# Five weight slots whose low part replaces the loaded block, unrolled stage loops, and other first transfers

## What is computed

```python
def swiglu(x, w_in, w_out):
    gate, up = jnp.split(x @ w_in, 2, axis=-1)
    return (jax.nn.silu(gate) * up) @ w_out
...
    x = x + 0.5 * swiglu(rmsnorm(x, ffn1_norm_g[l]), ffn1_w_in[l], ffn1_w_out[l])
```

## Time and profile before

| | |
|---|---|
| median of 3 runs | 1616.91 us (1616.56 to 1619.34) |
| the profiled execution's own time | 1615.48 us |
| its span, first to last instruction | 1613.8 us |
| TensorE busy | 1598.9 us, 99% |
| VectorE busy | 1220.4 us, 76% |
| ScalarE busy | 806.4 us, 50% |
| weight loads, 1 MB each | 269 on SyncE's queue, median 4.9 us from issue to landing |
| modulation loads, 1 MB each | 72 on GpSimd's queue, median 7.5 us |
| params, consts | 1474 KB, 280.5 KB |

### The profile page before, as it was taken

The page is one execution under the profiler, slowest core; times in us unless marked ns, Lnnn a source line. Parts: engine busy times, 40 slices in busy tenths (PEclk is TensorE's granted clock), DMA queues, the critical chain, the costliest instruction groups (busy, mean ns, idle before and its releaser), DMA issues.

```text
span 1613.8 us, 33803 instructions
## 1 busy us (share of the span) xinstructions
PE 1598.9 (99%) x14163; PEld 1577.0 (98%) x14163; DVE 1220.4 (76%) x1382; ACT 806.4 (50%) x892; POOL 48.2 (3%) x81
## 2 busy tenths in 40 slices
PE   9999999999999999999999999999999999999998
PEld 9999999999999999999998999999999998899998
DVE  7788786676778878887768788867889578774544
ACT  5434567654644354444567554345443456654343
POOL 0000000000000000000000000000000010000000
PEclk9999999999999999999999999999999999999999
DMA  8788644444568865888343369874898545345551
GB/s 334 282 305 306 225 178 170 150 157 160 182 258 291 314 229 206 334 320 310 140 176 131 131 238 343 309 284 157 297 339 322 187 144 196 132 157 209 182 199 61
DMA packets 51067, 365.04 MB, mean 226 GB/s; under 512 B 5793, under 2 KB 5921, under 8 KB 7073
## 3 DMA queue, kind: packets, MB, share of 16 engines
q1 hardware_dynamic: 40176, 287.03, 48.9%
q0 software_dynamic: 10368, 75.50, 12.9%
q10 hardware_dynamic: 432, 1.20, 0.2%
HBM read 362.65 MB, written 1.05 MB: 225 GB/s over the span
## 4 chain that ended last, share of the span: by engine, by line
PE 95%; DVE 2%; ACT 1%; DMA 1%; issue 1%; DVEq 0%; SPq 0%; ACTq 0%
PE bank L261 53%; PE bank L319 27%; PE bank L283 3%; PE bank L302 2%; PE bank L253 1%; PE bank L2172 1%; PE bank L406 1%; DVE wlo L192 1%; PE bank L417 1%; DMA raw<-stream_in 0%; PE bank L1675 0%; PE bank L2218 0%; PE bank L2124 0%; PE bank L2142 0%; PE bank L451 0%
## 5 line engine op out<-in xcount | busy, mean ns | idle before, releaser
L192 DVE TENSOR_TENSOR wlo<-raw,whi 128x2048 fp32r<-128x2048 f32 x254 | 581.0, 2289 | 187.0 <-ACT whi L184 186.3
L261 PE MATMUL bank<-xh,whi 128*128 128x256 f32 x2544 | 707.6, 278 | 1.6 <-DVE wlo L192 1.6
L261 PE MATMUL bank<-xh,wlo 128*128 128x256 f32 x2544 | 704.1, 277 | 0.0
L261 PE MATMUL bank<-xl,whi 128*128 128x256 f32 x2544 | 704.0, 277 | 0.0
L184 ACT ACTIVATE whi<-raw 128x2048 fp32r<-128x2048 f32 x253 | 482.5, 1913 | 260.4 <-PE bank L261 147.7
L261 PEld LDWEIGHTS bank<-xh,whi 128*128 128x128 f32 x2544 | 478.2, 188 | 3.1 <-DVE wlo L192 2.0
L261 PEld LDWEIGHTS bank<-xl,whi 128*128 128x128 f32 x2544 | 478.0, 188 | 0.1
L261 PEld LDWEIGHTS bank<-xh,wlo 128*128 128x128 f32 x2544 | 477.9, 188 | 0.0
L319 PE MATMUL bank<-hid_hi,whi 128*128 128x256 f32 x1056 | 293.3, 278 | 0.0
L319 PE MATMUL bank<-hid_hi,wlo 128*128 128x256 f32 x1056 | 292.2, 277 | 0.0
L319 PE MATMUL bank<-hid_lo,whi 128*128 128x256 f32 x1056 | 292.2, 277 | 0.0
(11 more groups left out here) (398 smaller groups left out, 1904.7 us busy)
## 6 DMA issues: line engine op xcount, KB each, us to landing
raw<-stream_in SPq DMA_DIRECT2D x269, 1024.0 KB, 4.9
mod_raw<-mod_in POOLq DMA_DIRECT2D x72, 1024.0 KB, 7.5
params<-params_in SPq DMA_DIRECT2D x1, 1474.0 KB, 9.1
x<-x_in SPq DMA_DIRECT2D x2, 512.0 KB, 4.3
raw<-stream_in SPq DMA_DIRECT2D x2, 512.0 KB, 6.5
m_gsu<-sgu_in ACTq DMA_DIRECT2D x1, 1024.0 KB, 4.8
y_out<-y_tiles SPq DMA_DIRECT2D x4, 256.0 KB, 2.9
consts<-consts_in SPq DMA_DIRECT2D x1, 280.5 KB, 7.2
```

What stands on the lines that cost most here:

```text
L192: dve.tensor_tensor(wlo[:, s, :], raw[:, s, :], whi[:, s, :].bitcast(F32), ALU.subtract)\
L261: last = pe.matmul(out[:, m, :], (whi, wlo)[wp][:, s, k * 256 + m * P:k * 256 + m * P + P], (xh, xl)[ap][:, k, :], start=(k == 0 and j == ...
```

## The change

- Five slots instead of three. `raw` and `wlo` lie in the same place: the low part is written over the loaded block. `whi` has its own place. 
- A load of block b into its slot now waits until TensorE has finished block b-5 (`w_used`), and no longer for the split of block b-3. ScalarE may round once block b-5 is finished.
- Six isn't a multiple of five, so the loops over turns on PE, ACT and DVE are written out, each turn with its own slots. SyncE's and GpSimd's loops stay.
- `mod_raw` is halved: two halves of one block, 512 KB each, with a semaphore each; half t is asked for when the step on the same half of the block before is done.
- In mix3 the packed low part gets other columns than the high part, since it is written over the loaded block, and `dve_split_q` makes its second piece wait for its first.
- In mix2 the output block 3 gets a `pe_apart`.
- Start: x and block 0 come whole; SyncE waits for x, asks for block 1, waits for block 0, and then asks for block 2, consts, block 3, params and block 4. ScalarE rounds blocks 0 and 1 in halves, VectorE splits block 1 in halves, and `pe_first_block` does the first four row tiles with both activation parts before the last four, without the twelve warming products.

```diff
-SLOTS = 3
+SLOTS = 5
...
-        raw = sb("raw", [P, SLOTS, BLK])
+        (raw,) = region(raw=([P, SLOTS, BLK], F32))
+        wlo = sb("wlo", [P, SLOTS, BLK], F32R)
         whi = sb("whi", [P, SLOTS, BLK], F32R)
-        wlo = sb("wlo", [P, SLOTS, BLK], F32R)
-        mod_raw = sb("mod_raw", [P, 2, BLK])
+        mod_raw = sb("mod_raw", [P, 2, D])
...
-            s = slot_of(n0)
+            s = slot_of(n0 + per * i)
...
-            for part, (w, xs) in enumerate(((whi, xh), (whi, xl), (wlo, xh))):
+            for part, k0, k1 in ((0, 0, 4), (1, 0, 4), (0, 4, 8), (1, 4, 8), (2, 0, 8)):
+                w, xs = ((whi, xh), (whi, xl), (wlo, xh))[part]
...
-            with pe.Fori(1, 5) as i:
+            for i in range(1, 5):
                 turn(i, False)
...
-                s = q % 2
-                dve.wait_ge(sem(f"mod_loaded{s}"), 16 * (2 * g0 + q // 2 + 1) + 32 * i)
                 for t in range(2):
                     k = 2 * q + t
+                    dve.wait_ge(sem(f"mod_loaded{t}"), 16 * (4 * g0 + q + 1) + 64 * i)
                     if k == 0:
-                        ins = dve.tensor_scalar(mod_acc[:, :], mod_raw[:, s, 0:D], c_act[:, 0:1], None, ALU.mult)
+                        ins = dve.tensor_scalar(mod_acc[:, :], mod_raw[:, 0, :], c_act[:, 0:1], None, ALU.mult)
...
-                pe_out(pe, F0 + MIX2_IN + b, hi, lo, b == 0, b == MIX2_OUT - 1, acc=MIX_ACC, beside=beside(MIX2_IN + b))
+                apart = lambda quarter: quarter == 0 and pe_apart(pe, ACC[3][:, 0:P])
+                pe_out(pe, F0 + MIX2_IN + b, hi, lo, b == 0, b == MIX2_OUT - 1, acc=MIX_ACC,
+                       beside=apart if b == 3 else beside(MIX2_IN + b))
...
-                ins = dve.tensor_tensor(q_parts(wlo, b)[i], q_parts(raw, b)[i], q_parts(whi, b)[i].bitcast(F32), ALU.subtract)
+                ins = dve.tensor_tensor(q_parts("lo", b)[i], q_loaded(b)[i], q_parts("hi", b)[i].bitcast(F32), ALU.subtract)
+                if i == 0:
+                    ins.then_inc(sem("m3_q_split"), 1)
+                    dve.wait_ge(sem("m3_q_split"), b - first_block[MIX3_AT] - UQ0 + 1)
...
-            for i in range(2):
-                sp.dma_start(x[:, 4 * i:4 * i + 4, :], a_x[:, 4 * i:4 * i + 4, :]).then_inc(sem(f"x_loaded{i}"), 16)
-            sp.dma_start(raw[:, 0, 0:H], a_stream[0:P, 0:H]).then_inc(sem("w_loaded_part"), 16)
-            sp.dma_start(raw[:, 0, H:BLK], a_stream[0:P, H:BLK]).then_inc(sem("w_loaded0"), 16)
-            sp.wait_ge(sem("x_loaded1"), 16)
-            for n in range(1, SLOTS):
-                sp.dma_start(raw[:, n, :], a_stream[n * P:n * P + P, :]).then_inc(sem(f"w_loaded{n}"), 16)
-                if n == 1:
-                    sp.dma_start(consts[:, :], a_consts).then_inc(sem("consts_loaded"), 16)
+            sp.dma_start(x[:, :, :], a_x[:, :, :]).then_inc(sem("x_loaded"), 16)
+            sp.dma_start(raw[:, 0, :], a_stream[0:P, :]).then_inc(sem("w_loaded0"), 16)
+            sp.wait_ge(sem("x_loaded"), 16)
+            sp.dma_start(raw[:, 1, :], a_stream[P:2 * P, :]).then_inc(sem("w_loaded1"), 16)
+            sp.wait_ge(sem("w_loaded0"), 16)
+            sp.dma_start(raw[:, 2, :], a_stream[2 * P:3 * P, :]).then_inc(sem("w_loaded2"), 16)
+            sp.dma_start(consts[:, :], a_consts).then_inc(sem("consts_loaded"), 16)
+            sp.dma_start(raw[:, 3, :], a_stream[3 * P:4 * P, :]).then_inc(sem("w_loaded3"), 16)
+            sp.dma_start(params[:, 4 * KD:P_N], a_params[:, 4 * KD:P_N]).then_inc(sem("params_loaded"), 16)
+            sp.dma_start(raw[:, 4, :], a_stream[4 * P:5 * P, :]).then_inc(sem("w_loaded4"), 16)
...
-                sp.wait_ge(sem("w_lo_ready"), s - SLOTS + 1 + SLOTS * turn)
+                sp.wait_ge(sem("w_used"), s - SLOTS + 1 + SLOTS * turn)
...
-            def load(s, turn):
-                pool.dma_start(mod_raw[:, s, :], a_mod[ds(s * P + 2 * P * turn, P), :])\
-                    .then_inc(sem(f"mod_loaded{s}"), 16)
+            def load(t, turn):
+                pool.dma_start(mod_raw[:, t, :], a_mod[ds(P * turn, P), t * D:t * D + D])\
+                    .then_inc(sem(f"mod_loaded{t}"), 16)
...
-                            pool.wait_ge(sem("mod_step"), 2 * s + 2 - 4 + 4 * turn)
-                            load(s, turn)
+                            pool.wait_ge(sem("mod_step"), t - 1 + 2 * turn)
+                            load(t, turn)
```

More of the change, by code:

```diff
@@ L104, in sem, with region @@
             return sems[name]
-        raw = sb("raw", [P, SLOTS, BLK])
+        def region(**tensors):
+            with ExitStack() as here:
+                return [here.enter_context(nc.sbuf_tensor(name, shape, dt)) for name, (shape, dt) in tensors.items()]
+        (raw,) = region(raw=([P, SLOTS, BLK], F32))
+        wlo = sb("wlo", [P, SLOTS, BLK], F32R)
         whi = sb("whi", [P, SLOTS, BLK], F32R)
-        wlo = sb("wlo", [P, SLOTS, BLK], F32R)
-        mod_raw = sb("mod_raw", [P, 2, BLK])
+        mod_raw = sb("mod_raw", [P, 2, D])
         mod_tab = sb("mod_tab", [P, 144])
@@ L137, in build_program @@
         cols = sb("cols", [P, 72])
-        def region(**tensors):
-            with ExitStack() as here:
-                return [here.enter_context(nc.sbuf_tensor(name, shape, dt)) for name, (shape, dt) in tensors.items()]
         gate, hid, hid_hi, hid_lo, mod_turned, mod_part, mod_acc = region(
@@ L173, in use_of @@
         def use_of(n0, i=0, per=0):
[L174 removed]
+            return (n0 + per * i) // SLOTS
         def act_split(act, n0, i=0, per=0):
@@ L209, in build_program @@
                 halves_index[n] = n_halves
-                n_halves += 1
+                n_halves += 2 if n == 0 else 1
         def act_split_halves(act, n):
@@ L805, in act_ffn_later @@
             turn(0, True)
-            with act.Fori(1, 5) as i:
+            for i in range(1, 5):
                 turn(i, False)
@@ L896, in dve_ffn_later @@
             turn(0, 0, False, True)
-            with dve.Fori(0, groups) as i:
+            for i in range(groups):
                 turn(i, 1, True)
             if groups < 4:
-                with dve.Fori(0, 4 - groups) as i:
+                for i in range(4 - groups):
                     turn(i, 1 + groups, False)
@@ L944, in act_ffn @@
             more = F0 + 33 < N_BLOCKS
-            with act.Fori(0, 4 + more) as i:
+            for i in range(4 + more):
                 turn(i, False)
@@ L1024, in dve_ffn @@
             if groups:
-                with dve.Fori(0, groups) as i:
+                for i in range(groups):
                     turn(i, True, False)
             if groups < 5:
-                with dve.Fori(groups, 4 + more) as i:
+                for i in range(groups, 4 + more):
                     turn(i, False, False)
@@ L2556, in _ @@
         def _(pool):
[L2558 to L2560 removed]
+            def load(t, turn):
+                pool.dma_start(mod_raw[:, t, :], a_mod[ds(P * turn, P), t * D:t * D + D])\
+                    .then_inc(sem(f"mod_loaded{t}"), 16)
             if N_GROUPS:
                 pool.wait_ge(sem("params_loaded"), 16)
[L2564 to L2565 removed]
+                for t in range(2):
+                    load(t, 0)
                 def turns(lo, hi):
                     with pool.Fori(lo, hi) as turn:
[L2569 to L2581 removed]
+                        for t in range(2):
+                            pool.wait_ge(sem("mod_step"), t - 1 + 2 * turn)
+                            load(t, turn)
+                before = 4 * sum(MOD_GROUPS[f] for kind, f, _ in phases[:5] if kind == "ffn")
+                turns(1, before + 1)
+                turns(before + 1, 4 * N_GROUPS)
             if any(kind == "mix3" for kind, _, _ in phases):
```

94 lines of the change are left out of this document (37 added, 57 removed).

## The result

The changed kernel takes 1720.9 us, the median of 4 runs (1718.1 to 1726.4); the kernel before beside it takes 1617.0. The ratio is 1.064, with a 95% interval of 1.0625 to 1.0655: 104 us slower. The forecast was 1649 with a range of 1614 to 1690. Its direction was right, its size was not: the loss is three times the forecast's 32 us and lies above the range.

A forecast was written before the change was run, and what follows sets the result against it. TensorE, busy 99%, bounds the kernel, with VectorE having little room in modulation stages. New TensorE waits of 34.2 us less 1.6 from small parts give +32.6, so 1649 us, range 1614 to 1690.

The forecast's parts named there:

- The new wait: VectorE waits for a modulation half ahead of each pair's second block; TensorE then waits for splits, 34.2 us in sum.
- The costs of nothing: Five slots with loads behind `w_used`, written-out loops and the in-place subtraction (2.29 us as before) each cost 0.
- S: VectorE's stall per pair of modulation blocks, waiting for a half load: 1.8 us in f2 to f4, 1.2 in f0, f1.
- the rooms: Stall time VectorE can absorb per FFN before TensorE waits: 7.05 us in f2, f3; 5.7 in f4; 1.8 in f0, f1.
- Half 1 at nothing more: Second modulation half, issued 1.3 us after the first and needed 1.3 us after it, adds no stall.
- Half the bytes, half the transfer: Modulation half's landing: 1.13 us taken off a 1 MB load's best 5.0, giving 3.9 us for 512 KB.
- Crowding +0.7: Added to the stall's lower end of 1.1 us, since a weight load meets about every second half load.
- crowding: Rival: loads on both queues collide as TensorE finishes blocks, stall per pair over 2.7 us; 1682 to 1714 us, chance 0.13.
- Start: First transfers: block 1 has the DMA engines to itself, so TensorE takes it at 15.7 instead of 17.2; gain 1.4 us.
- mix2: The added `pe_apart` product brings the last 144 products nearer 113 ns each; gain 0.5 us.
- The half loads fit: Rival: a half lands within 3.5 us of its issue, VectorE's spare time swallows the stalls; 1615 us, chance 0.13.
- More lead from five slots: Rival: ScalarE's roundings run ahead, the two 1.12 us waits per turn go; about 1615 us, chance 0.06.

The follow-up runs named there:

- e1: The changed kernel with the modulation in whole 1 MB blocks again, asked for as in the kernel before, and four weight slots: 1616.9 us, ratio 0.9989.
- e2: The kernel before with one edit, the modulation loaded in halves of 512 KB as in the change: 1699.7 us, ratio 1.0513.
- e4: The changed kernel with VectorE's modulation steps reading a constant piece of params without waiting, half loads still issued: 1615.3 us, ratio 0.9982.
- e9: The kernel before with the modulation in halves, each half contiguous in HBM: 1672.5 us, ratio 1.034.
- e10: The changed kernel with each modulation half contiguous in HBM: 1703.1 us, ratio 1.0524.
- e8: The changed kernel with weight loads also waiting for the split of the block three before, SyncE's loop written out: 1705.6 us, ratio 1.0553.
- e6_start_apart: The kernel before with only the change's first transfers, first-block order, halves of blocks 0 and 1, and mix2's added product: 1615.9 us, ratio 0.9985.

## Why the prediction was right and wrong

**Right: the place and the direction.** The new wait stands where the forecast put it, it holds up VectorE, TensorE waits for the splits behind it, and f5, which has no modulation, loses nothing. e1, e2 and e4 show it from three sides. TensorE waits 62.7 us for these splits, where the forecast looked for some 30. The costs of nothing hold too: five slots and loops (e1: 0.9989), the subtraction in place (2287 ns against 2289 in the page of before).

**The step that failed: the size of S, the stall per pair.** I took 1.8 us in f2 to f4 and 1.2 in f0 and f1; the page gives 85.1 / 24 = 3.5 and 29.8 / 12 = 2.5. With these in the forecast's own arithmetic: 8 x 3.5 = 28.4 less 7.05 is 21.3 each in f2 and f3, less 5.7 is 22.7 in f4; 6 x 2.5 = 14.9 less 1.8 is 13.1 each in f0 and f1; together 91.5, with the start 90. The profiled execution lost 102.6. So by this sum the rooms and the way from a stall to TensorE were about right, and S alone carries 57 of the 70 us that were missing. Three things in it were wrong:
- *Half 1 at nothing more.* This is the largest. Of VectorE's wait some 44 us stand ahead of second halves, which the forecast put at nothing, and 71 ahead of first ones, for which it had 24 x 1.8 + 12 x 1.2 = 58. A second half is asked for 1.3 us later and wanted 1.3 us later, but it lands 6.7 us after its issue at the median, a first half 5.2.
- *Half the bytes, half the transfer.* I took the transfer from 1 MB loads of whole rows and from the earlier trace rows, which is a store to HBM and no load. A half that takes 4 KB of every 8 goes slower; e9 puts that at 27 us of e2's 83, e10 at 18 of the change's 104. The lowest landing, estimated at 3.9 and measured at 3.9, was right by luck and hid this: 3.4 would have been the contiguous one.
- *Crowding +0.7 because a weight load meets every second half.* The weight load isn't met by chance. In e2 VectorE's split sets it free just ahead of the half, and the half stands behind it; in the change TensorE's finished block does, at a time that is worse still for the second half (e8: 15 us). And the earlier trace rows, which I quoted for TensorE's clock, had the DMA engines busy at 0.88 of the stretch; I didn't read that column.

The case itself was among the rivals, as "crowding" with S over 2.7 and 0.13; its price, up to 99 us, would have held nearly all of it. The range left it out for the most part.

**Where the other 13 us are, only argued.** The granted clock fell to its lower level (1.2 GHz) in eight places of the changed kernel, 27 us in all, one between f1 and f2 and seven in FFN stages with modulation, in which TensorE keeps waiting; both kernels have one more in their last microseconds, and before has no other. The stretches of two of them, the one between the stages first:

```profile
635.00:640.00 5.00, 5.00 (x49) 4.94 (x50) 2.40 (x8) 1.02 (x3) 0.00 (x0) 0.66 0.30 126
```
```profile
660.00:670.00 10.00, 8.29 (x73) 8.06 (x72) 5.79 (x5) 0.14 (x1) 1.06 (x2) 1.00 0.87 315
670.00:674.00 4.00, 3.85 (x20) 3.88 (x20) 2.19 (x4) 3.37 (x3) 0.00 (x0) 0.57 0.95 343
```

And after the waits the products often run at 118 ns instead of 113 with the granted clock at 1.00. In the chain of the changed kernel, in f2's turn without modulation, two blocks take 11.31 us where they took 10.88:

```profile
805.05 11.54 PE bank L260 x96
816.59 5.65 PE bank L318 x48
822.24 11.31 PE bank L260 x96
```

By the starts of its weight products the lower clock cost TensorE some 11 us, and the slower pace some 16 more than in the kernel before. In turns where VectorE sets the time both are hidden in TensorE's waits, as the chain of such a turn shows; behind the last such turn of an FFN they aren't. How much of the 13 us is the one or the other no run shows.

**Start: right in size, not in its path.** Block 1 begins at 15.62, forecast 15.7, before 17.20. The forecast had ScalarE's roundings set this, done at 14.4, and 1.2 us of half split behind them. ScalarE was done at 13.40 already. The chain of the changed kernel goes through VectorE, which is still busy with the split of block 0 and then makes both halves of block 1 without a pause. So the agreement to 0.1 us is in part luck.

```profile
11.10 2.20 DVE wlo L191
13.30 1.14 DVE wlo L809
14.44 1.15 DVE wlo L811
15.58 0.04 issue
15.62 5.73 PE bank L260 x48
```

**mix2, right; mix3, not to be told.** The last products of mix2 run at 113.9 ns now (132 of them in 15.04 us, where 144 took 16.96), and the stage is 0.4 us shorter in e1 and e4, forecast 0.5.

```profile
962.65 15.04 PE bank L318 x132
```

mix3 is 0.8 us longer in the changed kernel, but 0.7 in e6_start_apart too, which has mix3's old code.

**The rivals.** "The half loads fit" falls: even a contiguous half needs 3.3 to 3.4 us at best, just inside its bound of 3.5, and 4.7 to 5.3 at the median; the change's own halves need 3.9 at best. "More lead from five slots" falls: the 1.11 us waits for ScalarE's rounding are still in the turn (712.12 in the first timeline).

## What to carry to other kernels

A buffer's cycle is the step that reads it, the issue of the next load and its landing in the traffic of that very stage; when this comes near the time between two uses, the wait goes to the engine that reads, so halving a buffer wants the landing of the half as it will lie in HBM and in the queue, not half of the old one, and that of the second half as well as of the first. See what the program sets free just ahead of the load: here a 1 MB load that started a moment earlier went first. And where a stretch is quoted for its engines, read its DMA share as well.
